# A fused two-block layer on one core: the beginning reordered, and the steps of a recurrence issued one block later

## The chip, the cores and the metric

One core of a Trainium2 chip runs the whole computation in one launch. The metric is the device time of the launch in microseconds (us), the median of several runs of the same program. The engines are TensorE (PE; PEld is its weight load), VectorE (DVE), ScalarE (ACT), GpSimd (POOL), and SyncE (SP), whose queue issues the large transfers.

## The reference, cut to what matters

The kernel computes two residual blocks in turn, on 512 tokens of 1024 channels. The change lies in the first one:

```
x' = x * rsqrt(mean(x^2) + eps) * w ;  mod = silu(c) @ ada_w + ada_b  (shift, scale, gate)
h  = x' * (1 + scale) + shift
z  = h @ w_in                      -> u_pool, g_pool, q, f_pre, i_in, g_h (1024 columns each)
f  = lb + (1 - lb) * sigmoid(f_pre) ;  k = 1 - f
o  = gated linear recurrence over 512 steps in chunks of 64, 8 heads of 128 (q, log f, k, i_in)
o  = rms_norm(o) * silu(g_h)
pool = multi-window mean of u_pool, mixed by pool_w, times silu(g_pool)
y  = [pool, o] @ w_out ;  x + gate * rms_norm(y)
```

The second block (attention, convolutions, a gated feed-forward net) follows and is not touched.

## The kernel before, in words

Everything is written out by hand: five programs (`sp_prog` L623, `pool_prog` L662, `act_prog` L788, `dve_prog` L1410, `pe_prog` L2156), one for each engine, each a fixed order of instructions with waits on semaphores. No scheduler moves anything.

**The stream.** All weights come from one array, `wstream`, whose items `stream_layout` (L32) lists in order; SP fetches them one by one into places that `place` (L283) gives: four early buffers (`EARLY`), then three `RAW` buffers in rotation. SP waits until the last user of a place is done. An item is 1 MB: either two weight blocks ("w"), or two columns of 128 of a modulation matrix ("a"). Head 0 has ten items: eight of `ada_w` and two of weights (blocks 0 and 1; 2 and 3).

**Exact products.** An fp32 product is made of three fast ones. ScalarE rounds a weight block to its high part `WH` and VectorE subtracts to get the low part `WL` (`split`, L791 and L1413). The activations have the parts `HH` and `HL` alike. `mm3` then issues high x high, high x low, low x high. A block (1024 x 128 weights) is 8 x 3 = 24 products of 512 columns. Block nb+4 is split once block nb is done (`after`), so ScalarE and VectorE go in step with TensorE.

**The beginning.** Squares of x on ScalarE (tokens' tiles 0 and 2) and VectorE (1 and 3); GpSimd takes the power -1/2; ScalarE scales x (`XLT`); TensorE transposes it; VectorE sums the modulation's items against silu(c) (`dot`, a fused multiply and sum of 1024 elements; `first_dots` L1466, `scales` L1473); ScalarE applies the modulation (`modulated`, L892) and rounds (`h_high`, L898), VectorE takes the low part (`h_low_first`, L1481). For the first four channel tiles the products of blocks 0 to 3 are plain fp32 (`plain_tile`, L2232) on the unsplit weights, then come three-part products (`first_tile`, L2239). `awake` issues small products whose result is not used: `WARM` = (12, 8) of them in two places (L2210).

**The recurrence.** Block 4h+b is head h's input b: v (0), forget gate (1), q (2), output gate (3). `head` (L852) and `gates` (L843) on ScalarE empty their banks. Head h's recurrence is a list of steps from -8 to 22, written as `hgrn(h, step)` in each engine's program: -7 transposes v; -3 makes the first product on VectorE (`Q<-HB`) and the first scores; -2 to 3 scale keys and queries level by level (levels 2 to 7: VectorE's `HB<-HB,TOT` and `Q<-Q,TOT` in turn with ScalarE's copies `PTA`, `UPA`); 5 transposes the keys and makes the scores of the six levels on TensorE, which needs level 7; 6 merges the scores; 9 output and state products; 10 the states; 13 products with the states; 14 squares (ScalarE), 15 their scale, then GpSimd's power; 16 scales the output `XL` (ScalarE), 18 transposes it, 19 gates it (`XL<-PB`, VectorE).

Which step stands where is set by two functions. Each block has four places, t = 0 to 3, behind its second, fourth, sixth and eighth channel tile:

```
def tick_of(nb, t):
    return 4 * (nb - 4) + t if nb < B_POOL else 112 + 4 * POOL_TICKS.index(nb) + t

def heads_at(nb, t):
    return [(h, tick_of(nb, t) - 16 * h) for h in range(8) if -8 <= tick_of(nb, t) - 16 * h < 23]
```

All engines follow it. On VectorE the dots of later modulation items stand at fixed (nb, t) of their own (`DOTS`, L327). Head 0's steps -8 to -1 are issued ahead of that loop.

**The pool's start** (blocks 32 on). Blocks 34 and 35 are the inputs u of pool 3; GpSimd adds shifted copies (`pool_adds`, L719; `UPA<-UPA`), VectorE and ScalarE finish them (`tail`, L1608 and L957). The last steps of head 7 fall in these blocks. GpSimd's order is written with `recur(32, 33, 34)`, the adds of the first tile, `recur(35, 36)`, the adds of the second.

Of the kernel before, what the change touches and what calls it, by code (L numbers as in the profile page):

```python
# [5 lines left out]
F32 = mybir.dt.float32  # L6
# [8 lines left out]
D = 1024  # L15
# [16 lines left out]
def stream_layout():  # L32
# [16 lines left out]
    for h in range(8):  # L49
        if h == 0:  # L50
            items += first[0:3]
        w(("w_in", 0, 0, 8, [(I0 + h * 128, 128)]), ("w_in", 0, 0, 8, [(F0 + h * 128, 128)]))
        if h:
            also()
        else:
            items += first[3:4]
        w(("w_in", 0, 0, 8, [(Q_0 + h * 128, 128)]), ("w_in", 0, 0, 8, [(GH0 + h * 128, 128)]))
        if h:
            also()
        else:  # L60
            items += first[4:8]
# [221 lines left out]
def place(n):  # L283

    if n < NEARLY:
        return ("early", n), None
    if 7 <= n < 10:
        return ("early", n - 7), n - 7
    return ("raw", n % NRAW), None if n < 7 else n - 6 if n < 13 else n - NRAW
# [81 lines left out]
def build_in(nc, ctx, A, out, consts, masks):  # L371
# [244 lines left out]
    def tick_of(nb, t):  # L616
        return 4 * (nb - 4) + t if nb < B_POOL else 112 + 4 * POOL_TICKS.index(nb) + t
# [44 lines left out]
    def pool_prog(e):  # L662
# [48 lines left out]
        for step in range(-8, 0):  # L711
            hgrn(0, step)
# [697 lines left out]
    def dve_prog(e):  # L1410
        v = Eng(e)

        def split(nb):  # L1413

            if nb >= len(BLOCKS):
                return
            n, at, size = BLOCKS[nb]
            v.wait_ge(S_.a_w, nb)
            i = nb % NW
            v.tt(WL[i][:, 0:size], raw_of(n)[:, at:at + size], WH[i][:, 0:size].bitcast(F32), SUB).then_inc(S_.v_w, nb)  # L1420
# [36 lines left out]
        for i in (1, 3):
            v.wait_ge(S_.x[i // 2], "x")
            if i > 1:
                v.wait_ge(S_.v_s, ("xsq", 1))  # L1460
            v.dot(NORM2[2], XLT[:, i, :], XLT[:, i, :], MUL, sct(0)[:, i:i + 1], scale=1.0 / D).then_inc(S_.v_s, ("xsq", i))
# [115 lines left out]
        v.wait_ge(S_.a_s, "lt")  # L1577
        v.recip(OML, LT).then_inc(S_.v_s)
        v.wait_ge(S_.v_s)
        v.tt(LT, LT, OML, MUL).then_inc(S_.v_s)  # L1580
        v.wait_ge(S_.v_s)
        v.tt(LB, LT, LT, SUB).then_inc(S_.v_s)
        v.wait_ge(S_.v_s)
        v.ts(LT, LB, 1.0, None, SUB)
        v.ts(OML, LB, -1.0, 1.0, MUL, ADD).then_inc(S_.v_s, "lb")
# [7 lines left out]
        for step in range(-8, 0):  # L1593
            hgrn(0, step)
# [561 lines left out]
    def pe_prog(e):  # L2156
# [53 lines left out]
        WARM = (12, 8)  # L2210
# [569 lines left out]
```

## Time and profile before

| | |
|---|---|
| median of 3 runs | 1124.45 us (1122.73 to 1125.68) |
| profiled execution, its own time | 1123.52 us |
| its span | 1121.7 us |
| PE busy | 1094.9 us (98%) |
| DVE, ACT, POOL busy | 792.1 (71%), 550.9 (49%), 79.1 (7%) |
| transfers | 135.54 MB, 121 GB/s mean; 419 GB/s in the stretch 3 to 34 us |
| granted TensorE clock, mean | 0.995 |

Busy time says little of TensorE, since matmuls are pipelined and their ends are modelled: what can be won is in its idle stretches. The span is what the rows are counted in; the execution's own time is 1.8 us longer.

### The profile page before, as it was taken

The page shows a single profiled execution, that of the slowest core. Times are in us where ns is not written, and L with a number is a line of the kernel's source. Part 1 is how long each engine was busy: PE and PEld are TensorE (multiplying, and loading weights), DVE is VectorE, ACT ScalarE, POOL GpSimd, SP SyncE. Part 2 cuts the span into 40 slices and gives each one's busy share as a digit, 9 for nine tenths or more (in the row PEclk, how much of TensorE's full clock was granted, in tenths as well). Part 3 has the DMA queues.
Part 4 walks back from the last instruction along what each step waited for, and adds up shares of the span by engine and source line. Part 5 has one row for each costly group of instructions (what it writes and reads, how often), then busy time and mean ns, then how long its engine had stood idle before and what let it go on. Part 6 is the DMA issues. An engine that isn't in the chain of part 4 may idle for free.

```text
span 1121.7 us, 15071 instructions
## 1 busy us (share of the span) xinstructions
PE 1094.9 (98%) x6009; PEld 891.1 (79%) x6009; DVE 792.1 (71%) x1290; ACT 550.9 (49%) x968; POOL 79.1 (7%) x115
## 2 busy tenths in 40 slices
PE   7899999999999999999999999999999999999997
PEld 4578888888888888888867666778888888888886
DVE  5876889877677747667897899786656565645427
ACT  5666565556233437764256675555444444431311
POOL 0111100111321100101000002000000000000001
PEclk9999999999999999999999999999999999999999
DMA  9653333344255754131010211022222232352211
GB/s 379 237 195 144 142 123 120 145 169 176 99 214 196 276 207 146 44 122 55 29 50 1 75 45 69 4 110 97 99 105 106 82 113 75 113 181 101 76 39 75
DMA packets 22368, 135.54 MB, mean 121 GB/s; under 512 B 2545, under 2 KB 2969, under 8 KB 8474
## 3 DMA queue, kind: packets, MB, share of 16 engines
q1 hardware_dynamic: 19936, 128.46, 31.6%
q10 hardware_dynamic: 2362, 6.12, 1.6%
q8 instruction: 47, 0.77, 0.3%
q14 instruction: 23, 0.19, 0.1%
HBM read 132.45 MB, written 2.12 MB: 120 GB/s over the span
## 4 chain that ended last, share of the span: by engine, by line
PE 90%; DVE 4%; ACT 4%; issue 1%; DMA 1%; POOL 0%; DVEq 0%; ACTq 0%; POOLq 0%
PE PB L185 89%; PE PB L193 2%; ACT WH L199 1%; DVE WL L206 1%; DMA PC<-in_params 1%; DVE HL L206 1%; ACT L200 0%; DVE EARLY L1436 0%; ACT HH L199 0%; DVE XL L214 0%; ACT PTA L200 0%; DVE CV L214 0%; ACT XL L200 0%; DVE XL L218 0%; ACT HB L200 0%
## 5 line engine op out<-in xcount | busy, mean ns | idle before, releaser
L185 PE MATMUL PB<-HH,WH 128*128 128x512 f32 (+1 forms) x880 | 338.4, 385 | 6.2 <-ACT HB L199 2.5
L185 PE MATMUL PB<-HH,WL 128*128 128x512 f32 (+1 forms) x880 | 332.6, 378 | 0.0
L185 PE MATMUL PB<-HL,WH 128*128 128x512 f32 (+1 forms) x880 | 332.5, 378 | 0.0
L206 DVE TENSOR_TENSOR WL<-RAW,WH 128x1024 fp32r<-128x1024 f32 (+2 forms) x172 | 196.5, 1148 | 190.2 <-ACT WH L199 189.7
L199 ACT ACTIVATE WH<-RAW 128x1024 fp32r<-128x1024 f32 (+2 forms) x172 | 167.7, 980 | 285.8 <-PE PB L185 267.7
L185 PEld LDWEIGHTS PB<-HH,WH 128*128 128x128 f32 x880 | 165.5, 188 | 40.9 <-ACT HB L199 2.9
L185 PEld LDWEIGHTS PB<-HH,WL 128*128 128x128 f32 x880 | 165.5, 188 | 31.3
L185 PEld LDWEIGHTS PB<-HL,WH 128*128 128x128 f32 x880 | 165.7, 188 | 29.7 <-issue 0.5
L214 DVE SCALAR_TENSOR_TENSOR CV<-VP,PC,CV 128x512 f32<-128x512 f32 x120 | 88.1, 778 | 0.7
L185 PE MATMUL PB<-WL,AH 128*128 128x512 f32 (+1 forms) x198 | 72.4, 366 | 0.0
L185 PE MATMUL PB<-WH,AH 128*128 128x512 f32 (+1 forms) x198 | 72.4, 366 | 0.0
L185 PE MATMUL PB<-WH,AL 128*128 128x512 f32 (+1 forms) x198 | 72.4, 365 | 0.0
L1436 DVE CUSTOM_DVE_ANT_0 RAW<-RAW,CR,PC 128x1024 f32<-128x1024 f32 x48 | 60.5, 1279 | 0.0
L185 PE MATMUL PB<-WH,HH 128*128 128x512 f32 x128 | 51.6, 403 | 0.3 <-DVE HL L206 0.3
L185 PE MATMUL PB<-WH,HL 128*128 128x512 f32 x128 | 50.5, 395 | 0.0
L185 PE MATMUL PB<-WL,HH 128*128 128x512 f32 x128 | 50.4, 393 | 0.0
L214 DVE SCALAR_TENSOR_TENSOR PTA<-PB,PC,PTA 128x511 f32<-128x511 f32 x66 | 49.2, 747 | 1.2
L185 PE MATMUL PB<-PTA,VG 128*128 128x512 f32 x96 | 49.5, 599 | 0.2 <-ACT PTA L200 0.2
L185 PEld LDWEIGHTS PB<-WH,AH 128*128 128x128 f32 x198 | 37.4, 189 | 6.2
L185 PEld LDWEIGHTS PB<-WL,AH 128*128 128x128 f32 x198 | 37.4, 189 | 6.1
L185 PEld LDWEIGHTS PB<-WH,AL 128*128 128x128 f32 x198 | 37.3, 188 | 6.0
L206 POOL TENSOR_TENSOR PX<-PX,NPOW 128x1 f32<-128x1 f32 (+2 forms) x8 | 7.4, 922 | 458.9 <-DVE PX L206 420.5
(293 smaller groups left out, 1692.7 us busy)
## 6 DMA issues: line engine op xcount, KB each, us to landing
RAW<-in_wstream SPq DMA_DIRECT2D x101, 1024.0 KB, 4.9
EARLY<-in_wstream SPq DMA_DIRECT2D x7, 1024.0 KB, 13.0
RAW<-in_wstream SPq DMA_DIRECT2D x5, 768.0 KB, 4.4
RAW<-in_wstream SPq DMA_DIRECT2D x5, 512.0 KB, 3.4
XL<-in_x SPq DMA_DIRECT2D x2, 1024.0 KB, 6.6
HB<-in_x SPq DMA_DIRECT2D x2, 1024.0 KB, 5.9
out<-XL SPq DMA_DIRECT2D x8, 256.0 KB, 2.0
ROWS<-in_rows ACTq DMA_DIRECT2D x3, 512.0 KB, 7.6
```

The lines of the kernel that those rows point to most:

```text
L185: return self.put(lambda e: e.matmul(o, l, r, start=start, stop=stop, skip_group_check=skip))
L193: return self.put(lambda e: e.transpose(o, i, idn))
L199: return self.put(lambda e: e.activation(o, i, f))
L206: return self.put(lambda e: e.tensor_tensor(o, a, b, op))
L214: return self.put(lambda e: e.scalar_tensor_tensor(out=o, in0=a, scalar=s, in1=b, op0=o1, op1=o2))
L1436: v.put(lambda e: e.tensor_tensor_reduce(out=PROD if vec == "cc" else w, in0=w, in1=ROW[vec], scale=1.0, scalar=col(bias, j + i), op0=MUL, ...
```

## The change

It has these parts.

- Stream: the item with blocks 0 and 1 comes third instead of fourth; the item of blocks 2 and 3 stays sixth. One `place` is adapted.
- ScalarE's beginning: a Silu on a dummy element first (it brings the table), the first square of x before silu(c), the exponential for the bounds behind the squares; a dummy Sigmoid behind the fourth high part. VectorE's: the first square of x before the bounds, the rest of the bounds behind the first scales; dots and low parts in another order.
- Blocks 0 to 3 are split only in their second half (the first is used unsplit).
- ScalarE empties block 0's bank as soon as it is done, then splits block 4, then computes the gates.
- TensorE: 3 instead of 8 products in the second `awake`; the last three-part products of blocks 0 to 3 with all high parts of the activations first.
- All steps of the recurrence stand four places (one block) later, but for head 0's first ones.

```diff
@@ stream_layout
-            items += first[0:3]
+            items += first[0:2]
         w(("w_in", 0, 0, 8, [(I0 + h * 128, 128)]), ("w_in", 0, 0, 8, [(F0 + h * 128, 128)]))
...
-            items += first[3:4]
+            items += first[2:4]
@@ place
     if 7 <= n < 10:
-        return ("early", n - 7), n - 7
+        i = (0, 1, 3)[n - 7]
+        return ("early", i), i
@@ tick_of
-        return 4 * (nb - 4) + t if nb < B_POOL else 112 + 4 * POOL_TICKS.index(nb) + t
+        return 4 * (nb - 5) + t if nb < B_POOL else 108 + 4 * POOL_TICKS.index(nb) + t
@@ in the programs of POOL, ACT, DVE, PE
-        for step in range(-8, 0):
+        for step in range(-8, -4):
             hgrn(0, step)
@@ act_prog, split (and the same in dve_prog)
-            a.copy(WH[nb % NW][:, 0:size], raw_of(n)[:, at:at + size]).then_inc(S_.a_w, nb)
+            lo_ = 512 if nb < NW else 0
+            a.copy(WH[nb % NW][:, lo_:size], raw_of(n)[:, at + lo_:at + size]).then_inc(S_.a_w, nb)
@@ act_prog, beginning
-        a.wait_ge(S_.par, "par")
-        a.wait_ge(S_.v_s, "lt")
-        a.act(LT, LT, ACTF.Exp).then_inc(S_.a_s, "lt")
+        a.wait_ge(S_.g_s, "npow")
+        a.act(NM[:, 9:10], NPOW[:, 0:1], ACTF.Silu)
...
+        x_squares(0)
         for c in range(2):
             a.wait_ge(S_.p_sm, ("c", c))
             op = a.act(ROW["c"][:, 512 * c:512 * c + 512], main.of(("z", 0, 2 + c)), ACTF.Silu)
         op.then_inc(S_.a_s, "c")
...
+        x_squares(2)
+        a.wait_ge(S_.v_s, "lt")
+        a.act(LT, LT, ACTF.Exp).then_inc(S_.a_s, "lt")
...
         h_high(2)
         h_high(3)
+        a.act(NM[:, 10:11], NPOW[:, 0:1], ACTF.Sigmoid)
...
-        Vb, Kb, Bb, Qb, Gb = head_bufs(0)
+        head(0, 0)
         split(NW)
-        a.wait_ge(S_.p_blk, 1)
-        gates(0)
-        head(0, 0)
+        head(0, 1)
+        head(0, 2)
         split(NW + 1)
-        head(0, 2)
         split(NW + 2)
@@ dve_prog, beginning
+        x_squares(1)
         v.wait_ge(S_.par, "par")
...
         first_dots(1, 0)
+        first_dots(1, 1)
+        scales(1)
         split(0)
         split(1)
-        first_dots(1, 1)
-        scales(1)
-        split(2)
         first_dots(2, 0)
         first_dots(2, 1)
         scales(2)
+        split(2)
         split(3)
         h_low_first(4)
-        first_dots(3, 0)
+        dot(FIRST_ADA[6], 0, "c")
         h_low_first(5)
+        dot(FIRST_ADA[6], 1, "c")
         first_dots(3, 1)
         scales(3)
-        h_low_first(6, 7, 0, 1, 2, 3)
+        h_low_first(0, 1, 6, 2, 7, 3)
@@ pe_prog
-        WARM = (12, 8)
+        WARM = (12, 3)
...
-        for p, bs in ((2, (0, 1)), (2, (2, 3)), (3, (1, 0)), (3, (2, 3))):
-            for k in (2 * p, 2 * p + 1):
+        for bs in ((0, 1), (2, 3)):
+            for k in (4, 5):
                 for b in bs:
                     first_tile(b, k)
+        for bs in ((1, 0), (2, 3)):
+            for k in (6, 7):
+                pe.wait_ge(S_.a_h, ("h", k))
+                for b in bs:
+                    pe.mm(zs[b], WH[b][:, js(k)], hh(k), False, False)
+                    pe.mm(zs[b], WL[b][:, js(k)], hh(k), False, False)
+            for k in (6, 7):
+                pe.wait_ge(S_.v_h, ("h", k))
+                for b in bs:
+                    op = pe.mm(zs[b], WH[b][:, js(k)], hl(k), False, k == 7)
```

Three places show what the table of steps does to an engine's order.

VectorE from the splits of blocks 5 to 7 on, before. `Q<-HB` is head 0's first product, `HB<-HB` and `Q<-Q` its levels, `RAW,PX` a dot, `WL<-RAW` a split:

```order
L206 TENSOR_TENSOR WL<-RAW,WH 128x1024 x3
L206 TENSOR_TENSOR Q<-HB 128x512
L206 TENSOR_TENSOR HB<-HB 128x256
L206 TENSOR_TENSOR Q<-Q,HB 128x256
L206 TENSOR_TENSOR HB<-HB,TOT 128x128x2
L206 TENSOR_TENSOR Q<-Q,TOT 128x128x2
L234 COPY_PREDICATED AT<-MK,PB 128x512
L206 TENSOR_TENSOR HB<-HB,TOT 128x64x4
L206 TENSOR_TENSOR Q<-Q,TOT 128x64x4
```

The same place with the change:

```order
L206 TENSOR_TENSOR WL<-RAW,WH 128x1024 x3
L206 TENSOR_TENSOR Q<-HB 128x512
L1442 ISA RAW,PX<-RAW,GP,PC 128x1024
L1442 ISA PX 128x1
L206 TENSOR_TENSOR HB<-HB 128x256
L206 TENSOR_TENSOR Q<-Q,HB 128x256
L206 TENSOR_TENSOR HB<-HB,TOT 128x128x2
L206 TENSOR_TENSOR Q<-Q,TOT 128x128x2
L234 COPY_PREDICATED AT<-MK,PB 128x512
L1442 ISA RAW,PX<-RAW,GP,PC 128x1024
L1442 ISA PX 128x1
L206 TENSOR_TENSOR WL<-RAW,WH 128x1024
```

Two dots and the split of block 8 now stand ahead of level 4 (`128x64x4`), which follows the last row.

ScalarE, around the gate of head 0 (the Silu behind the table load, then two rows of the modulation, then the split of block 8), before:

```order
L199 ACTIVATE UPA<-HB 128x8x32
L199 ACTIVATE UPA<-Q 128x8x32
L200 ACT_TABLE_LOAD
L200 ACTIVATE HB<-PB 128x512
L200 ACTIVATE XL<-XL 128x1024
L200 ACTIVATE CR<-CR 128x1024
L199 ACTIVATE WH<-RAW 128x1024
```

With the change:

```order
L199 ACTIVATE PTA<-HB 128x64x4
L199 ACTIVATE PTA<-Q 128x64x4
L200 ACT_TABLE_LOAD
L200 ACTIVATE HB<-PB 128x512
L200 ACTIVATE XL<-XL 128x1024
L200 ACTIVATE CR<-CR 128x1024
L199 ACTIVATE WH<-RAW 128x1024
L199 ACTIVATE HB<-PB 128x512
L199 ACTIVATE UPA<-HB 128x32x8
```

The group stood behind the last copies of the levels (`128x8x32`) and stands now behind level 3's (`128x64x4`), in front of the rest.

ScalarE at the pool's start, before. `UPA<-PB` empties a block u, `XR,SCT<-PB` are head 7's squares, `XL<-PB,SCT` its scaling, `DH<-UPA` the tail of a pool tile, `GP<-PB` a gate:

```order
L199 ACTIVATE UPA<-PB 128x512
L200 ACTIVATE XL<-PB,SCT 128x128 x4
L199 ACTIVATE WH<-RAW 128x256
L200 ACTIVATE GP<-PB 128x512
L199 ACTIVATE DH<-UPA 128x512
```

With the change:

```order
L199 ACTIVATE UPA<-PB 128x512
L197 ACTIVATE XR,SCT<-PB 128x128 x4
L199 ACTIVATE WH<-RAW 128x256
L200 ACTIVATE GP<-PB 128x512
L199 ACTIVATE DH<-UPA 128x512
L200 ACTIVATE XL<-PB,SCT 128x128 x4
```

The scaling stood ahead of the second tile's tail and stands behind it; the squares moved from ahead of the first tile's tail to behind it.

## Rows read from the trace of the kernel before

**Rows 1.** The page's chain of waits that ended last, by engine.

```profile
PE 90%; DVE 4%; ACT 4%; issue 1%; DMA 1%; POOL 0%; DVEq 0%; ACTq 0%; POOLq 0%
```

**Rows 2.** Issues: SP's timeline (start, length), and issues with KB and us to landing.

```profile
16.37 0.33 SPq L182 DMA_DIRECT2D EARLY<-in_wstream  x1
...
EARLY<-in_wstream SPq DMA_DIRECT2D x1, 1024.0 KB, 12.9
...
RAW<-in_wstream SPq DMA_DIRECT2D x1, 1024.0 KB, 4.7
```

**Rows 3.** Timelines of DVE and ACT, head 0: start, us, engine, line, operation [idle].

```profile
60.82 0.41 DVE L206 TENSOR_TENSOR HB<-HB,TOT 128x256 f32<-128x256 f32 x1
61.79 0.42 DVE L206 TENSOR_TENSOR HB<-HB,TOT 128x256 f32<-128x256 f32 x1 [0.22 <-ACT UPA L199]
62.47 1.28 DVE L1436 CUSTOM_DVE_ANT_0 RAW<-RAW,GP,PC 128x1024 f32<-128x1024 f32 x1
69.66 1.23 DVE L206 TENSOR_TENSOR WL<-RAW,WH 128x1024 fp32r<-128x1024 f32 x1 [3.04 <-ACT WH L199]
...
64.89 1.28 ACT L200 ACT_TABLE_LOAD   x1
68.58 1.05 ACT L199 ACTIVATE WH<-RAW 128x1024 fp32r<-128x1024 f32 x1
```

**Rows 4.** Timeline of DVE, the scales of channels 4, 5 and of 6, 7.

```profile
34.39 0.16 DVE L214 SCALAR_TENSOR_TENSOR PX<-PX,PC 128x2 f32<-128x2 f32 x1
42.34 0.16 DVE L214 SCALAR_TENSOR_TENSOR PX<-PX,PC 128x2 f32<-128x2 f32 x1
```

**Rows 5.** Timelines of ACT and PE, from the last high part to block 4.

```profile
44.73 0.63 ACT L199 ACTIVATE HH<-AT 128x512 fp32r<-128x512 f32 x1
49.03 1.28 ACT L200 ACT_TABLE_LOAD   x1
52.91 1.05 ACT L199 ACTIVATE WH<-RAW 128x1024 fp32r<-128x1024 f32 x1
...
53.06 0.50 PE L185 MATMUL PB<-HH,WH 128*128 128x512 f32 x1 [2.49 <-ACT HB L199]
```

**Rows 6.** Timeline of PE, blocks 4 and 5, and head 0's transposes.

```profile
57.82 0.40 PE L185 MATMUL PB<-HL,WH 128*128 128x512 f32 x1
...
64.19 0.39 PE L185 MATMUL PB<-HH,WL 128*128 128x512 f32 x1
65.13 0.66 PE L193 MATMUL PB<-IDN,HB 128*128 128x128 f32 x4 [0.55 <-DVE HB L206]
```

**Rows 7.** Stretches: us, busy of each engine, PEclk, DMA share, GB/s.

```profile
18.00:22.00 4.00, 3.72 (x17) 3.07 (x18) 3.33 (x7) 3.43 (x5) 0.00 (x0) 0.57 1.01 422
52.00:54.00 2.00, 0.94 (x4) 0.81 (x5) 0.83 (x2) 2.00 (x4) 1.23 (x3) 1.00 0.02 4
704.00:708.00 4.00, 4.00 (x12) 3.08 (x12) 3.59 (x14) 2.59 (x4) 1.33 (x1) 0.57 0.00 0
```

**Rows 8.** Timelines of DVE and PE, head 3: its last level and its transposes.

```profile
184.48 0.41 DVE L206 TENSOR_TENSOR HB<-HB,TOT 128x256 f32<-128x256 f32 x1
...
186.26 0.60 PE L193 MATMUL PB<-IDN,HB 128*128 128x128 f32 x4
```

**Rows 9.** Timelines of PE, ACT and POOL, head 7 at the pool's start.

```profile
293.76 1.09 PE L185 MATMUL PB<-SS,E 128*64 128x128 f32 x14
301.71 0.60 PE L193 MATMUL PB<-IDN,XL 128*128 128x128 f32 x4
...
294.89 0.28 ACT L197 ACTIVATE XR<-PB 128x128 f32<-128x128 f32 x1 [2.13 <-PE PB L185]
300.31 1.14 ACT L200 ACTIVATE XL<-PB,SCT 128x128 f32<-128x128 f32 x4
...
297.98 1.02 POOL L206 TENSOR_TENSOR SCT<-SCT,NPOW 128x4 f32<-128x4 f32 x1
300.49 4.69 POOL L206 TENSOR_TENSOR UPA<-UPA 128x512 f32<-128x512 f32 x4 [1.50 <-ACT UPA L199]
```

More of the change, by code:

```diff
@@ L876, in act_prog, with x_squares @@
         a.dma(IDN[:, :], consts[:, 0:128]).then_inc(S_.idn, "idn", by=16)
-        a.wait_ge(S_.par, "par")
-        a.wait_ge(S_.v_s, "lt")
-        a.act(LT, LT, ACTF.Exp).then_inc(S_.a_s, "lt")
+        a.wait_ge(S_.g_s, "npow")
+        a.act(NM[:, 9:10], NPOW[:, 0:1], ACTF.Silu)
+        def x_squares(i):
+            a.wait_ge(S_.x[i // 2], "x")
+            a.act(NORM2[i // 2], XLT[:, i, :], ACTF.Square, scale=2.0 ** -5, acc=sct(0)[:, i:i + 1]).then_inc(S_.a_s, ("xsq", i))
+        x_squares(0)
         for c in range(2):
@@ L883, in act_prog @@
         op.then_inc(S_.a_s, "c")
-        for i in (0, 2):
-            a.wait_ge(S_.x[i // 2], "x")
-            a.act(NORM2[i // 2], XLT[:, i, :], ACTF.Square, scale=2.0 ** -5, acc=sct(0)[:, i:i + 1]).then_inc(S_.a_s, ("xsq", i))
+        x_squares(2)
+        a.wait_ge(S_.v_s, "lt")
+        a.act(LT, LT, ACTF.Exp).then_inc(S_.a_s, "lt")
         for i in range(4):
@@ L927, in act_prog @@
         a.dma(ROW["c2"], A["rows"][:, 2 * D:3 * D]).then_inc(S_.crow, "cr", by=16)
-        Vb, Kb, Bb, Qb, Gb = head_bufs(0)
+        head(0, 0)
         split(NW)
-        a.wait_ge(S_.p_blk, 1)
-        gates(0)
-        head(0, 0)
+        head(0, 1)
+        head(0, 2)
         split(NW + 1)
-        head(0, 2)
         split(NW + 2)
         split(NW + 3)
-        for step in range(-8, 0):
+        for step in range(-8, -4):
             hgrn(0, step)
@@ L1418, in split @@
             v.wait_ge(S_.a_w, nb)
-            i = nb % NW
-            v.tt(WL[i][:, 0:size], raw_of(n)[:, at:at + size], WH[i][:, 0:size].bitcast(F32), SUB).then_inc(S_.v_w, nb)
+            i, lo_ = nb % NW, 512 if nb < NW else 0
+            v.tt(WL[i][:, lo_:size], raw_of(n)[:, at + lo_:at + size], WH[i][:, lo_:size].bitcast(F32), SUB).then_inc(S_.v_w, nb)
         def after(nb):
@@ L1451, in lo, with x_squares @@
             v.tt(dst, src, hi.bitcast(F32), SUB).then_inc(S_.v_h, name)
+        def x_squares(i):
+            v.wait_ge(S_.x[i // 2], "x")
+            v.dot(NORM2[2], XLT[:, i, :], XLT[:, i, :], MUL, sct(0)[:, i:i + 1], scale=1.0 / D).then_inc(S_.v_s, ("xsq", i))
+        x_squares(1)
         v.wait_ge(S_.par, "par")
@@ L1456, in dve_prog @@
         v.tt(LT, hlb, hlb, SUB).then_inc(S_.v_s, "lt")
[L1457 to L1461, printed above, removed]
+        v.wait_ge(S_.v_s, ("xsq", 1))
+        x_squares(3)
         v.wait_ge(S_.a_s, ("xsq", 2))
@@ L1487, in dve_prog @@
         scales(0)
+        v.wait_ge(S_.a_s, "lt")
+        v.recip(OML, LT).then_inc(S_.v_s)
+        v.wait_ge(S_.v_s)
+        v.tt(LT, LT, OML, MUL).then_inc(S_.v_s)
+        v.wait_ge(S_.v_s)
+        v.tt(LB, LT, LT, SUB).then_inc(S_.v_s)
+        v.wait_ge(S_.v_s)
+        v.ts(LT, LB, 1.0, None, SUB)
+        v.ts(OML, LB, -1.0, 1.0, MUL, ADD).then_inc(S_.v_s, "lb")
         first_dots(1, 0)
+        first_dots(1, 1)
+        scales(1)
         split(0)
         split(1)
-        first_dots(1, 1)
-        scales(1)
-        split(2)
         first_dots(2, 0)
@@ L1496, in dve_prog @@
         scales(2)
+        split(2)
         split(3)
         h_low_first(4)
-        first_dots(3, 0)
+        dot(FIRST_ADA[6], 0, "c")
         h_low_first(5)
+        dot(FIRST_ADA[6], 1, "c")
         first_dots(3, 1)
         scales(3)
-        h_low_first(6, 7, 0, 1, 2, 3)
+        h_low_first(0, 1, 6, 2, 7, 3)
         def hgrn(h, step):
@@ L1575, in hgrn @@
                     .then_inc(S_.v_ax, ("dg", h))
[L1577 to L1585, printed above, removed]
         first = LATER_ADA[0]
+        split(NW)
         dot(first, 0, "c")
-        split(NW)
         dot(first, 1, "c")
@@ L1592, in dve_prog @@
             split(NW + n)
-        for step in range(-8, 0):
+        for step in range(-8, -4):
             hgrn(0, step)
@@ L2242, in first_tile @@
             pe.wait_ge(S_.v_h, ("h", k))
-            op = pe.mm3(zs[b], wh[:, js(k)], wl[:, js(k)], hh(k), hl(k), False, k == 7)
-            if k == 7:
-                op.then_inc(S_.p_blk, b)
+            pe.mm3(zs[b], wh[:, js(k)], wl[:, js(k)], hh(k), hl(k), False, False)
         pe.wait_ge(S_.c, "c")
@@ L2267, in pe_prog @@
                 x_tiles(6, 7)
-        for p, bs in ((2, (0, 1)), (2, (2, 3)), (3, (1, 0)), (3, (2, 3))):
-            for k in (2 * p, 2 * p + 1):
+        for bs in ((0, 1), (2, 3)):
+            for k in (4, 5):
                 for b in bs:
                     first_tile(b, k)
+        for bs in ((1, 0), (2, 3)):
[8 more added lines that the diff above has]
+                    op = pe.mm(zs[b], WH[b][:, js(k)], hl(k), False, k == 7)
+                    if k == 7:
+                        op.then_inc(S_.p_blk, b)
         def hgrn(h, step):
@@ L2346, in tick @@
                     if nb == 4 and t == 0:
-                        for step in range(-8, 0):
+                        for step in range(-8, -4):
                             hgrn(0, step)
```

## The prediction, on record before the changed kernel ran

> **What bounds the kernel now.** The view of the chain that ended last comes first: TensorE (PE) carries 90% of it, VectorE (DVE) and ScalarE (ACT) 4% each [rows 1]. The change adds and removes next to no TensorE work, so it can only move waits of TensorE. The timelines of each engine show where these are. The first 38 us are preparation: x, norm, modulation. Then come the four products of head 0 (blocks 0 to 3), and from 53.06 us on the stream of blocks, where TensorE is never idle but for short gaps. I read the timelines in the order of the three edits: the beginning, the recurrence of head 0, and the end of the recurrence at head 7.
>
> **Part 1, the beginning.** Both reorderings of x (ScalarE's first square before its tables, VectorE's first square before the bounds) bring the norm's scale about 3 us forward. That alone ends nothing: the later channels wait for the modulation weights, which land one after another. The fifth pair to be summed needs the item that landed 12.9 us after its issue at 16.37, at 29.3 us [rows 2]. Its place in the stream is unchanged and the queue in front of it is as long, so it lands at 29.3 again. In the kernel before VectorE was behind it: two dots of 1.28 us, 2.4 for both since they overlap a little [rows 3], and the scales at 34.39 [rows 4]. After, VectorE has lost work ahead of it (half of the first four splits, halves of 1.22 us) and waits for the landing: 29.3 + 2.4 + 0.2 = 31.9. From there to the last scales it was 42.34 - 34.39 = 7.95 us [rows 4], and the moved halves and low parts make it 7.9 in my count. So the modulation is done 2.5 us earlier, and ScalarE's last high part, which started at 44.73 and took 0.63 [rows 5], ends at 42.86. TensorE has no work left when it comes: the second weights land two items (2.5 us each, 1 MB at some 420 GB/s) before 29.3, at 24.3, and the 16 plain products start the second pair then. They wait about 1.2 us for it, end near 35.5, and the 24 products of channels 4 and 5 near 41. Behind that high part stand 20 products (4 high, 4 low, 12 of the other pair). The pace is (64.19 - 57.82) / 28 = 0.2275 us [rows 6]; 20 of them and a restart are 4.65. The first four blocks end at 47.6 where they ended at 53.06 - 2.49 = 50.57 [rows 5]: **3.0 us earlier**.
>
> Block 4 waited those 2.49 us because ScalarE split block 4, loaded a table and computed the gates before it emptied the first bank. From the load at 49.03 to the split of block 5 at 52.91 are 3.88 us [rows 5]: 1.28 the load, 2.6 gates and copy. The change moves the table load to an idle place and empties the bank first. Block 0 ends with the eighth of the 20 products and is seen done at 45.1; copy 0.5, split 0.95, VectorE's low part 1.22 with two hand-overs of 0.1 give 48.0. TensorE waits 0.4 us instead of 2.49, and block 4 starts **5.1 us earlier**.
>
> **Part 2, the recurrence of head 0, one block later.** Before, TensorE reached the transposes of head 0 at 65.13, in the middle of block 5, after a wait of 0.55 [rows 6]. Now they stand in the middle of block 6, 24 products later, so 65.13 + 24 x 0.2275 = 70.6 is the time that would be no gain. TensorE could be there at 48.0 + 60 x 0.2275 + 1.2 (four transposes, the first scores, restarts) = 62.9. VectorE decides whether it may go on. Its order has three new things in front of the last factors: the first dot of the next item right behind head 0's first product, a second dot, and the split of block 8.
> The chain: from 45.1, copy, split, gates, copy (0.5 + 0.95 + 2.1 + 0.5) and the split of block 5 end at 50.2 on ScalarE; VectorE's part ends at 51.5 and frees the buffer of the next item. This lands 4.7 us after its issue [rows 2], at 56.2. The dot ends at 57.5. Levels 2 and 3 with ScalarE's copies take 2.2: one level is 61.79 - 60.82 = 0.97 [rows 3]. At 59.7 ScalarE turns to head 0's gate: table load, Silu, two rows of 1024, and only then the split of block 8, 68.58 - 64.89 = 3.69 us later [rows 3]. In the kernel before that stood behind the recurrence's factors and cost nothing. So the split runs from 63.4 to 64.45, VectorE's part starts 1.08 behind its start as at 69.66 [rows 3] and gives way to level 4 at 65.6. Three levels at 0.97 and one product of 0.42 end at 69.0. **TensorE waits 6.1 us in block 6 and goes on at 69.05, 1.5 us earlier than no gain.** Of the 5.1 us and of head 0's own waits that the shift was to save, all but 1.5 are given back.
> **A rule weighed.** The load at 64.89 is 1.28 us, and the 3.69 us to the split hold just it and the three activations, so 1.3 stands in the chain [rows 3]. The Trainium skill (ScalarE: Activation LUTs, What ACT_TABLE_LOAD costs) gives a switch a drain of about 1.4 us more, 2.66 in all. By it the wait would be 7.5 and nearly nothing of the gain be left. The trace has no such drain.
>
> **The clock.** An idle TensorE loses its clock here: the granted clock was 0.57 in 18 to 22 us, behind the wait for x, and in 704 to 708; it stayed 1.00 around the 2.49 us of block 4 [rows 7]. Such a mean is a stretch at the lower level, 1.2 GHz, and the rest at 2.4. A wait of 6.1 us is over twice the longest that kept it, so I expect the fall. At 704 to 708 the share lost is 4 x (1 - 0.57) = 1.7 us [rows 7]. Here the first 3.4 us are small score products; bounds 0.4 (they don't feel it) and 3.0 (the low level outlasts them). I take 1.5, as in the nearest row.
> The same rows bear on the warm-up products cut from 8 to 3. The Trainium skill (TensorE: Matmul & The Clock Gate, Part 1) says that the low clock is the default and activity lifts it, which speaks against the cut. The first plain tiles at half rate would cost up to 1.7 us; 1.2 of it falls in the wait for the second weights, so 0 to 0.6, taken as 0.
>
> **Part 3, heads 1 to 6.** Head 3's last factor ended at 184.48 + 0.41, TensorE came at 186.26: 1.4 us of room [rows 8]. The new order puts a table load and Silu (1.8 us) between levels 3 and 4 where there were none; the same order lets levels 1 to 3 run 0.5 to 0.7 earlier, since one dot less stands before them. Left is 0.2 us of room in heads 2 to 5, and 1.2 more in heads 1, 6 and 7, which have no dot between levels 5 and 6. Cost 0; bounds 0 and 1.
>
> **Part 4, head 7 at the pool's start.** Here the shift crosses an order that was not shifted. The chain before: state products at 293.76, squares 294.89, GpSimd's power 297.98 (1.02), its adds for the second pool tile 300.49 (4.69), and ScalarE's scaling at 300.31 (1.14), all ahead of the transposes at 301.71, which waited for nothing [rows 9]. GpSimd's adds and the scaling were side by side. After, the power of head 7 stands ahead of the adds as before, but ScalarE's scaling stands behind the tail that waits for these adds. So, from the end of the state products (293.76 + 1.09 in the old count [rows 9]): squares 1.1, sum 0.3, power 1.05, adds 4.7, VectorE's tail 0.9, ScalarE's copy 0.6 (512 columns, as the 0.63 at 44.73 [rows 5]), scaling 1.15: 9.8 us. TensorE does 12 products, and 18 of the next block, 30 x 0.2275 + 0.1 = 6.9 us. **A new wait of 2.8 us**; bounds 2 and 3.5, by what of the small ends overlaps.
>
> **Sum**, against the profiled execution of 1123.52: -1.5 + 1.5 + 0 + 2.8 = +2.8. That execution is 0.9 under the median of 1124.45. On the median it is 1127.2. A measurement of this kernel can't tell less than 0.3% (3.4 us) from no change, so below 1121.1 is faster and above 1127.8 slower; my forecast is the upper end of "same".
>
> **Rivals.**
> A, the beginning's gain is kept (0.15): VectorE isn't held in front of level 4. For it: ScalarE has idle stretches then, and the items may land earlier. Against: both engines work in order. With no wait in block 6 it gains 70.6 - 62.95 = 7.6, loses 2.8: 1119.6.
> B, the wait of head 7 doesn't come (0.16), since GpSimd's adds finish sooner or the order hides them: 1124.4, no change. Against it stand five durations in rows.
> C, slower by the clock (0.12): the low level lasts the full 3.0 in block 6 and also comes in head 7's wait of 2.8 us, another 1.7. It decides once that wait is longer than what keeps the clock; 2.49 kept it once. 1124.45 - 1.5 + 3.0 + 2.8 + 1.7 = 1130.4.
> D, slower by heads 2 to 5 (0.10): the 0.2 us of room is my count. If the dot between levels 5 and 6 falls fully into the path, each loses 1.0: 1131.
> E, the forecast (0.47), 1126.1 to 1128.7 by the clock's bounds.
> Faster is A: 0.15. Slower is C, D and a third of E: 0.37. The rest, 0.48, is no change. The range 1120.0 to 1130.5 leaves out the far parts of A and D.
>
> **What would show it.** Block 4 starts near 48 us. TensorE's longest wait is one of about 6 us near 63 to 69 for VectorE's HB product, and behind it the granted clock is 0.50. The waits of heads 1 to 6 are under 0.3. Near 307 us TensorE waits 2.8 us for ScalarE's XL. If block 6 has no such wait, the forecast is wrong on the fast side; if heads 2 to 5 show waits of 0.5 or more, on the slow side.

## The result, and the profile after

The changed kernel takes **1131.84 us** (median of 4 runs, 1131.43 to 1134.19) against 1124.97 us for the kernel before (4 runs beside it, 1122.73 to 1125.68). The ratio is 1.0069, 95% interval 1.0049 to 1.0089: slower by 0.7%. The prediction was 1127.2 with a range to 1130.5. The result lies above it, 0.8 over rival D's time and 1.4 over rival C's. By its mechanism it is nearest to C, as shown below.

The profiled execution took 1131.85 us with a span of 1130.0; its span is 8.3 us longer than that of before. The page's chain of waits that ended last, by engine, answers to [rows 1]:

```profile
PE 81%; DVE 7%; ACT 5%; DMA 3%; issue 2%; POOL 1%; SPq 0%; DVEq 0%; ACTq 0%; POOLq 0%
```

TensorE's share has fallen from 90% to 81%: the chain now leaves it in several places. The timeline of PE (start, length, engine, line, operation, and in brackets the idle time before it with what ended it) shows them, rows from the beginning to the pool's start:

```profile
47.83 0.47 PE L185 MATMUL PB<-HH,WH 128*128 128x512 f32 x1 [0.26 <-DVE WL L206]
52.32 0.69 PE L185 MATMUL PB<-HB 128*64 128x64 f32 x16 [1.04 <-ACT HB L199]
...
69.39 1.11 PE L193 MATMUL PB<-IDN,HB 128*128 128x128 f32 x4 [5.27 <-DVE HB L206]
70.44 2.78 PE L185 MATMUL PB<-PTA 128*64 128x32 f32 x48
73.02 2.75 PE L185 MATMUL PB<-UPA 128*64 128x32 f32 x48
75.71 0.80 PE L185 MATMUL PB<-HH,WH 128*128 128x512 f32 x1
76.30 0.63 PE L185 MATMUL PB<-HL,WH 128*128 128x512 f32 x1
...
80.57 0.55 PE L185 MATMUL PB<-HH,WL 128*128 128x512 f32 x1
80.95 0.40 PE L185 MATMUL PB<-HH,WH 128*128 128x512 f32 x1
...
282.49 0.65 PE L193 MATMUL PB<-IDN,XL 128*128 128x128 f32 x4 [0.88 <-ACT XL L200]
...
314.88 0.66 PE L193 MATMUL PB<-IDN,XL 128*128 128x128 f32 x4 [2.90 <-ACT XL L200]
...
379.79 0.47 PE L185 MATMUL PB<-WH,MPH 128*128 128x512 f32 x1 [0.29 <-DVE HB L214]
```

The same timeline of before has these rows around head 0:

```profile
56.87 0.69 PE L185 MATMUL PB<-HB 128*64 128x64 f32 x16 [1.71 <-ACT HB L199]
...
68.63 0.50 PE L185 MATMUL PB<-HH,WH 128*128 128x512 f32 x1
...
71.48 0.39 PE L185 MATMUL PB<-HH,WH 128*128 128x512 f32 x1
```

- Block 4 starts at 47.83 where it started at 53.06 [rows 5]: 5.2 us are won.
- The waits up to head 0's transposes were 1.71 (before the first scores at 56.87) and 0.55 [rows 6]; they are 1.04 and 5.27: 4.05 us are lost.
- From the transposes to the product behind the scores are 75.71 - 69.39 = 6.32 us, and the next 12 products take until 80.95: 5.24 us. Before it was 3.50 (65.13 to 68.63) and 2.85 (68.63 to 71.48). 5.2 us are lost without any wait.
- 0.9 us at 282.49 (head 6), 2.9 at 314.88 (head 7), 0.3 at 379.79.

Together -5.2 + 4.05 + 5.2 + 0.9 + 2.9 + 0.3 = +8.15 of the 8.3. Where the 5.2 us without a wait went is seen in the clock. The stretches of after (us, busy of each engine, PEclk, DMA share, GB/s):

```profile
18.00:22.00 4.00, 4.00 (x14) 2.03 (x15) 2.87 (x5) 2.52 (x5) 0.00 (x0) 1.00 1.00 418
64.00:66.00 2.00, 0.13 (x1) 0.00 (x0) 1.15 (x2) 1.30 (x2) 0.00 (x0) 1.00 0.73 307
66.00:68.00 2.00, 0.00 (x0) 0.00 (x0) 1.57 (x6) 1.33 (x4) 0.00 (x0) 0.81 0.00 0
78.00:80.00 2.00, 2.00 (x6) 1.61 (x5) 1.13 (x2) 0.00 (x0) 0.00 (x0) 0.50 0.03 8
80.00:82.00 2.00, 2.00 (x8) 1.58 (x8) 0.00 (x0) 0.79 (x1) 0.00 (x0) 0.78 0.77 246
```

The granted clock falls to 0.50 (1.2 GHz) in the wait, near 67.2, and comes back near 80.9, after 11.5 us of unbroken work. In it a product of 512 columns takes (80.57 - 76.30) / 10 = 0.427 us instead of 0.2275. The Trainium skill (TensorE: Matmul & The Clock Gate, Part 1) gives 426.7 ns for such a product at the low clock; the trace agrees. At 18 to 22 us the clock is 1.00 where it was 0.57 [rows 7]: the five warm-up products less cost nothing that shows here. x also comes earlier, and no run separates the two.

### The profile page after: what moved, and what is told of

Same layout as the page of the kernel before. It is cut to its first block, busy times and chain, and to the rows that moved or that the text cites. A ratio compares the mean times of both kernels' runs of the same rounds, so it can differ in the third digit from the quotient of the medians.

```text
span 1130.0 us, 15053 instructions
## 1 busy us (share of the span) xinstructions
PE 1097.8 (97%) x5999; PEld 891.9 (79%) x5999; DVE 792.1 (70%) x1290; ACT 550.4 (49%) x970; POOL 83.2 (7%) x115
## 4 chain that ended last, share of the span: by engine, by line
PE 81%; DVE 7%; ACT 5%; DMA 3%; issue 2%; POOL 1%; SPq 0%; DVEq 0%; ACTq 0%; POOLq 0%
PE PB L185 80%; DMA RAW<-in_wstream 3%; PE PB L193 2%; ACT WH L199 1%; DVE RAW L1442 1%; POOL UPA L206 1%; DVE WL L206 1%; DVE EARLY L1442 1%; ACT HH L199 0%; DVE XL L214 0%; SPq L182 0%; ACT L200 0%; DVE UPA L214 0%; DVE HB L206 0%; ACT PTA L200 0%
## 5 line engine op out<-in xcount | busy, mean ns | idle before, releaser
L206 DVE TENSOR_TENSOR WL<-RAW,WH 128x1024 fp32r<-128x1024 f32 (+3 forms) x172 | 195.6, 1144 | 199.3 <-ACT WH L199 198.7
L199 ACT ACTIVATE WH<-RAW 128x1024 fp32r<-128x1024 f32 (+3 forms) x172 | 166.6, 975 | 281.4 <-PE PB L185 270.5
## 6 DMA issues: line engine op xcount, KB each, us to landing
EARLY<-in_wstream SPq DMA_DIRECT2D x7, 1024.0 KB, 13.7
```

The source lines that it names most:

```text
L199: return self.put(lambda e: e.activation(o, i, f))
L206: return self.put(lambda e: e.tensor_tensor(o, a, b, op))
```

## Why the wait in block 6 is 5.3 us

VectorE and ScalarE up to the last factor of head 0 (timelines of DVE and ACT of after):

```profile
56.62 1.28 DVE L1442 CUSTOM_DVE_ANT_0 RAW<-RAW,GP,PC 128x1024 f32<-128x1024 f32 x1 [1.81 <-DMA RAW<-in_wstream]
64.85 1.23 DVE L206 TENSOR_TENSOR WL<-RAW,WH 128x1024 fp32r<-128x1024 f32 x1 [3.40 <-ACT WH L199]
65.99 0.42 DVE L206 TENSOR_TENSOR HB<-HB,TOT 128x256 f32<-128x256 f32 x1
68.92 0.42 DVE L206 TENSOR_TENSOR HB<-HB,TOT 128x256 f32<-128x256 f32 x1 [0.22 <-ACT UPA L199]
...
60.09 1.28 ACT L200 ACT_TABLE_LOAD   x1
61.38 0.60 ACT L200 ACTIVATE HB<-PB 128x512 f32<-128x512 f32 x1
63.77 1.04 ACT L199 ACTIVATE WH<-RAW 128x1024 fp32r<-128x1024 f32 x1
```

VectorE waits 1.81 us for an item, then 3.40 us for ScalarE's split of block 8, which stands behind the gate group of head 0 (60.09 to 63.77: 3.68 us). The four levels behind it are in time only at 69.34. This is the chain that the prediction worked out, within 0.4 us. Behind the load the Silu starts 0.01 us after its end; the drain that the Trainium skill (ScalarE: Activation LUTs, What ACT_TABLE_LOAD costs) adds does not show here either.

## The experiments

All were run in five rounds beside the kernel before, whose median was 1123.88 (e1 to e4), 1123.76 (e5 to e8) and 1123.68 us (e9, e10).

**e1: the steps back in their places, the new beginning kept.**

```diff
-        return 4 * (nb - 5) + t if nb < B_POOL else 108 + 4 * POOL_TICKS.index(nb) + t
+        return 4 * (nb - 4) + t if nb < B_POOL else 112 + 4 * POOL_TICKS.index(nb) + t
-        for step in range(-8, -4):
+        for step in range(-8, 0):
```

> The changed kernel with the recurrence's steps back in their old places; the new beginning is kept. Theory (the later steps make the loss, the beginning is a gain): block 4 starts at 47.8 us as in the changed kernel, head 0's transposes come in block 5 near 59 us (48.87 + 9.8 of TensorE work, VectorE's last factor held by the item that lands at 56.6), against 65.13 before, and no wait over 0.3 us stands in the pool's first blocks. Time 1119.5, between 1118 and 1122, that is 5.5 under before. Rival (the new beginning is paid back later by itself: half splits, the table loads, the moved item): 1124 to 1126.

Measured: 1120.52 (1118.51 to 1122.22, 6 runs), ratio 0.9968 [0.9957, 0.9980]. **Faster than before by 0.3%.** The timeline of PE:

```profile
47.85 0.47 PE L185 MATMUL PB<-HH,WH 128*128 128x512 f32 x1 [0.27 <-DVE WL L206]
52.35 0.69 PE L185 MATMUL PB<-HB 128*64 128x64 f32 x16 [2.46 <-ACT HB L199]
61.56 0.66 PE L193 MATMUL PB<-IDN,HB 128*128 128x128 f32 x4 [1.46 <-DVE HB L206]
...
368.57 0.47 PE L185 MATMUL PB<-WH,MPH 128*128 128x512 f32 x1 [0.41 <-DVE HB L214]
```

Of the 5.2 us at block 4 head 0 takes 1.6 back (61.56 against 65.13: 3.6 are left). Its transposes come 2.6 us later than the 59 that I expected, since the first scores wait 2.46 us and the transposes 1.46. At the first product of the mixes (`PB<-WH,MPH`, where the pool's tiles are mixed) 3.0 us are left (368.57 against 371.56), and by the medians 3.4 at the end. The profiled span is 4.3 us shorter, but in this run the clock did not fall near 704 as it did before [rows 7]. So the beginning is a gain, and the loss belongs to the steps.

**e2: the kernel before with only the steps later** (the lines of e1 the other way round).

> The kernel before with only the recurrence's steps one block later. Theory: the same three waits as in the changed kernel: block 6 (TensorE is there at 69.4, VectorE's last factor near 72.8: 3.4 us), head 6 in block 33 (0.9), head 7 in block 37 (2.9), and the clock, which costs nothing if 3.4 us keep it and up to 5.0 if they do not. 1124.97 + 2.9 + 4.2 = 1132 with the clock kept, 1137 with it lost. Rival (the steps are harmless by themselves and only collide with the new beginning): 1125.

Measured: 1135.48 (1134.33 to 1135.73, 4 runs), ratio 1.0099 [1.0086, 1.0112]. The timeline of PE:

```profile
73.06 1.12 PE L193 MATMUL PB<-IDN,HB 128*128 128x128 f32 x4 [4.54 <-DVE HB L206]
...
285.16 0.66 PE L193 MATMUL PB<-IDN,XL 128*128 128x128 f32 x4 [0.88 <-ACT XL L200]
317.56 1.04 PE L193 MATMUL PB<-IDN,XL 128*128 128x128 f32 x4 [2.90 <-ACT XL L200]
```

The same three waits. The first is 4.54 where I worked out 3.4, and the clock is lost with it. The transposes of 0.66 that take 1.04 at 317.56 show that here it is lost at head 7 too. The steps alone cost 11.6 us and the beginning alone gains 3.4: the sum is 8.2, the two together measured 6.9 to 8.0 more than before (by which median of before is taken). By these medians the two parts hardly touch each other.

**e3: the gate group behind the level copies.** ScalarE's `head(0, 3)` (load, Silu, two rows) moves behind the copies of block 5.

```diff
                 recur(4 * h + b)
-                if b == 0:
+                if b == (1 if h == 1 else 0):
                     head(h - 1, 3)
```

> The changed kernel with ScalarE's group for head 0's output gate (table load, Silu, two rows) behind the level copies of block 5 and behind the split of block 8. Theory (the group holds the split of block 8 and so level 4, and the clock falls because of the wait that this makes): the wait in block 6 shrinks from 5.27 to about 1.7 us, the granted clock stays 1.00 from 60 to 90 us, and 3.6 + 5.0 = 8.6 us come back: 1123.3, between 1121.5 and 1125. Rival (the item that lands at 56.6 and the dot that waits for it make the wait): the wait stays over 4 us, the clock falls, and the time is 1130 or more.

Measured: 1125.45 (1123.00 to 1127.86, 12 runs), ratio 1.0011 [1.0000, 1.0022]. The wait is as expected, the clock is not. PE and the stretches behind it:

```profile
66.05 0.66 PE L193 MATMUL PB<-IDN,HB 128*128 128x128 f32 x4 [1.77 <-DVE HB L206]
```

```profile
66.00:68.00 2.00, 1.95 (x38) 1.78 (x38) 0.33 (x1) 1.99 (x3) 0.00 (x0) 0.79 0.00 0
68.00:70.00 2.00, 2.00 (x43) 2.00 (x42) 0.00 (x0) 2.00 (x3) 0.00 (x0) 0.50 0.00 0
```

Five of the twelve runs had a mean clock of 0.997 and took 1123.00 to 1123.31, the 1123.3 of the theory. The other seven had 0.992 to 0.995 and took 1124.83 to 1127.86. The profiled one is among them: in it the clock fell after a wait of only 1.77 us, and again at head 7's wait, from 309 to 313. The transposes, the scores and the 12 products behind them took 9.45 us (66.05 to 75.50), where before took 6.35: 3.1 us for the first fall. So the group made 3.5 of the 5.27 us, and the clock's price is paid or not from run to run.

**e4: the wait filled with products whose result is not used.**

```diff
                 bk = take_aux(("kt", h), 0)
+                for _ in range(22 if h == 0 else 0):
+                    pe.mm(bk[:, :], WH[2][:, js(0)], hh(0), True, True)
```

> The changed kernel with 22 products of 512 columns, whose result is not used, in front of head 0's transposes: TensorE is busy for 5.0 of the 5.27 us that it waits. Theory (the idle stretch makes the clock fall, and that costs 5.0 us: transposes, scores and 12 products at about half pace until 80.9): the wait shows as 0.3 us, the granted clock stays 1.00, 1131.84 - 5.0 = 1126.9. My prediction took 1.5 for it: 1130.3. Rival (the clock falls because transposes and small scores follow, whatever stands before them): it falls all the same, 1131.8.

Measured: 1128.24 (1126.64 to 1129.76, 5 runs), ratio 1.0037 [1.0025, 1.0049]. PE, then its stretches:

```profile
69.50 0.65 PE L193 MATMUL PB<-IDN,HB 128*128 128x128 f32 x4 [0.34 <-DVE HB L206]
...
309.86 1.02 PE L193 MATMUL PB<-IDN,XL 128*128 128x128 f32 x4 [2.91 <-ACT XL L200]
```

```profile
68.00:70.00 2.00, 1.66 (x10) 1.04 (x8) 1.52 (x4) 1.77 (x4) 0.00 (x0) 1.00 0.00 0
74.00:76.00 2.00, 2.00 (x10) 1.62 (x10) 1.97 (x3) 0.16 (x1) 1.84 (x3) 1.00 0.86 356
...
310.00:312.00 2.00, 2.00 (x8) 1.71 (x8) 1.77 (x4) 0.00 (x0) 0.00 (x0) 0.50 0.00 0
312.00:314.00 2.00, 2.00 (x7) 1.60 (x6) 0.88 (x2) 0.46 (x1) 0.00 (x0) 0.65 0.26 33
```

The transposes come no earlier (69.50 instead of 69.39), and yet 3.6 us are won. The transposes and scores are the same as in after and the clock holds through them, so in block 6 it is the idle stretch that makes it fall. The missing 1.4 of the 5.0 us stand at head 7: there the clock falls now, for 2 x 0.50 + 2 x 0.35 = 1.7 us. The one run with a mean clock of 0.997 took 1126.64, near the 1126.9 of the theory; by its mean it kept the clock there, though no trace of it was kept.

**e5: head 7's scaling ahead of the pool's tail** (ScalarE).

```diff
             pool_gate(p, 0, nb)
+            recur(nb + 1)
             tail(p + 1, 1)
-            recur(nb + 1)
```

> The changed kernel with ScalarE's scaling of head 7 ahead of the tail of the second pool tile (recur(37) before tail(3, 1)). Theory (the scaling waits only because it stands behind the tail, which waits for GpSimd's adds): the wait of 2.9 us near 315 is gone, and with it the occasional fall of the clock there. 1131.84 - 2.9 = 1128.9, between 1127.5 and 1129.5. Rival (the power or GpSimd's queue makes the wait): it stays, 1131.8.

Measured: 1131.21 (1130.57 to 1132.08, 5 runs), ratio 1.0068 [1.0054, 1.0082]. The wait of 2.9 us is gone and the time hardly moved. It comes back further on, by the timeline of PE:

```profile
346.69 0.47 PE L185 MATMUL PB<-HH,WH 128*128 128x512 f32 x1 [0.52 <-DVE WL L206]
352.75 0.47 PE L185 MATMUL PB<-HH,WH 128*128 128x512 f32 x1 [0.36 <-DVE WL L206]
372.86 0.47 PE L185 MATMUL PB<-HH,WH 128*128 128x512 f32 x1 [0.81 <-DVE WL L206]
379.14 0.47 PE L185 MATMUL PB<-WH,MPH 128*128 128x512 f32 x1 [0.56 <-DVE HB L214]
```

2.25 us of new waits for VectorE, where after had the one of 0.29. From head 6's transposes at 282 to the first product of the mixes it takes 96.96 us (282.18 to 379.14), where after took 97.30. My expectation of 1128.9 was wrong by a second bound that stood just under the first.

**e6: e3 with 6 products of the kind of e4** (22 becomes 6), so that 0.4 us of the 1.77 are left.

> The gate group behind block 5's copies, as in e3_gate_behind, and 6 products with unused result in front of head 0's transposes, so that of the 1.77 us of waiting 0.4 is left. In e3 five runs of twelve had a mean clock of 0.997 and took 1123.0 to 1123.3, seven had 0.992 to 0.995 and took 1124.8 to 1127.9. Theory (even 1.8 us of waiting, followed by small products, puts the clock at risk; filled, it does not): most runs at 0.995 or higher, median 1123.3, spread under 2.5 us, what is left of it from the 2.9 us of head 7. Rival (the falls are chance or come elsewhere): the same two groups, median 1125.5.

Measured: 1124.35 (1122.86 to 1126.09, 11 runs), ratio 1.0006 [0.9997, 1.0015]. The spread is 3.2 us instead of 4.9, and three runs in eleven reach 0.997. The median is 1.1 under that of e3, half of what I expected: in the profiled run the clock held in block 6 and fell at head 7's 2.90 us instead, as in e4.

**e7: four orders mended.** e3 and e5, and besides VectorE's dot that waits for the item at 56.6 behind levels 2 and 3, and head 6's scaling ahead of the table load.

```diff
@@ VectorE
-                    dots(nb, t)
+                    if (nb, t) == (4, 3):
+                        dots(4, 1)
+                    if (nb, t) != (4, 1):
+                        dots(nb, t)
@@ ScalarE, block 32 (and the step left out in block 33)
             if m == 0:
+                hgrn(6, 16)
                 head(7, 3)
```

> The changed kernel with four orders mended: gate group behind block 5's copies, VectorE's dot of the item that lands at 56.6 behind levels 2 and 3, head 6's scaling ahead of the table load in block 32, head 7's ahead of the tail. Theory: none of the waits of 5.3, 0.9 and 2.9 us is left, the clock stays 1.00 from 24 us on, 1131.84 - 5.3 - 5.0 - 0.9 - 2.9 = 1117.7, between 1116.5 and 1119.5: 6.5 under before, more than the beginning with the old steps (1120.5). Rival (a dot held back delays the stream, or the table load now stands in another head's way): over 1120.

Measured: 1122.02 (1121.78 to 1123.68, 11 runs), ratio 0.9989 [0.9980, 0.9997]. That is 4.3 us more than expected. Head 0's wait is down to 0.66 and the clock holds through it. Head 6's wait of 0.88 is gone, but head 7's transposes now wait 0.78: ScalarE's scaling, load and Silu (from 268.53 on) hold its split of a block until 271.46, VectorE waits 2.56 us for it, and the last levels stand behind that. So that move won 0.1 us. The pool's stages show the waits of e5 again, and GpSimd's timeline shows where they start:

```profile
64.92 0.66 PE L193 MATMUL PB<-IDN,HB 128*128 128x128 f32 x4 [0.66 <-DVE HB L206]
...
277.54 0.63 PE L193 MATMUL PB<-IDN,HB 128*128 128x128 f32 x4 [0.78 <-DVE HB L206]
...
363.52 0.47 PE L185 MATMUL PB<-HH,WH 128*128 128x512 f32 x1 [0.83 <-DVE WL L206]
369.97 0.47 PE L185 MATMUL PB<-WH,MPH 128*128 128x512 f32 x1 [0.76 <-DVE HB L214]
```

```profile
296.90 1.02 POOL L206 TENSOR_TENSOR SCT<-SCT,NPOW 128x4 f32<-128x4 f32 x1 [5.93 <-DVE SCT L211]
297.89 4.79 POOL L206 TENSOR_TENSOR UPA<-UPA 128x512 f32<-128x512 f32 x4
```

The input of the adds (`UPA<-UPA`) was in place at 293.07 + 0.58 (ScalarE's copy of the block). GpSimd stands in front of head 7's power for 5.93 us and starts them 4.2 us late. In the profiled run the clock also fell for 6.8 us near 701, twice as long as in the kernel before (see the last section). Then VectorE's tail, dots, the fetch that the dots release, the splits and the gates of the mixes follow one another.

**e8: ScalarE's order around block 4 as before, on top of e1** (no Sigmoid in the pause; split, gates with the load, then block 0's bank).

> The kernel with the steps back (e1_steps_back, 1120.52), and in addition ScalarE's order around block 4 as before: split of block 4, the table load, the gates, then block 0's bank, and no Sigmoid in the pause. Theory (that order made 2.1 us of the 5.2 us by which block 4 starts earlier): block 4 starts at 49.9 instead of 47.85, the wait before it is 2.3 us. Head 0's transposes come later by less, since they waited 1.46 us there: 1120.5 to 1122.6, taken as 1121.8. Rival (the wait moves and nothing is lost): 1120.5.

Measured: 1121.23 (1120.65 to 1122.81, 11 runs), ratio 0.9979 [0.9970, 0.9988]. Block 4 starts at 50.09 behind a wait of 2.43 us, 2.2 later than in e1, and head 0's transposes come at 62.14, only 0.6 later. The order is worth 2.2 us at block 4 and 0.6 to 0.7 in the end.

**e9: e7 with GpSimd's adds ahead of head 7's power.**

```diff
                 if p == 3 and m == 1:
-                    recur(35, 36)
+                    recur(35)
                 if p == 2 and m == 0:
-                    recur(37)
+                    recur(36, 37)
```

> The kernel of e7_all_orders (1122.0, where 1117.7 was expected), and GpSimd's adds for the second pool tile ahead of head 7's power. In e7 these adds could start at 293.65 and start at 297.89, since GpSimd stands waiting for head 7's sum; VectorE's tail, its dots, the fetch behind them (4.7 us) and the splits follow in one chain, and TensorE waits 0.42, 0.35, 0.83 and 0.76 us for it from 337 to 370. Theory (the pool stages have a second bound right under TensorE, and the later steps lengthen it by these 4.3 us): the waits between 300 and 380 are gone, 1122.0 - 2.4 = 1119.6, between 1118 and 1120.5. Rival (the waits come from the stream itself, which cannot bring the items sooner): they stay, 1122.

Measured: 1120.23 (1118.67 to 1120.58, 5 runs), ratio 0.9962 [0.9948, 0.9976]. GpSimd's timeline:

```profile
293.79 4.68 POOL L206 TENSOR_TENSOR UPA<-UPA 128x512 f32<-128x512 f32 x4 [2.76 <-ACT UPA L199]
298.42 1.02 POOL L206 TENSOR_TENSOR SCT<-SCT,NPOW 128x4 f32<-128x4 f32 x1
```

TensorE has no wait of 0.3 us left from 278 to 467 us; the 0.78 at 277.6 stays, and so does head 0's, now 0.64. With the orders mended the later steps are no longer slower: 1120.2, the same as the 1120.5 of e1. In the profiled runs e9 is even 1.8 us ahead at the first product of the mixes (366.77 against 368.57), and loses more than that near 700, where its clock falls for 6.8 us and that of e1 does not. So whether the later steps, in good order, gain anything isn't shown.

**e10: after with both orders at head 7** (e5 and the lines of e9).

> The changed kernel with both orders at head 7 mended: ScalarE's scaling ahead of the tail (e5_head7_order alone: 1131.2, its wait of 2.9 us gone and 2.3 us of waits for VectorE's splits and gates in its place, 346 to 380), and GpSimd's adds ahead of the power. Theory: none of the two kinds of wait is left, 1131.84 - 2.9 - 0.3 = 1128.6, between 1127.8 and 1129.3. Rival (the waits behind 340 have another source): 1131.

Measured: 1128.08 (1127.28 to 1129.72, 5 runs), ratio 1.0039 [1.0026, 1.0051]. ScalarE's order alone brought 0.6 us, both together 3.8. The low stretch of the clock in block 6 was shorter here (back at 78.1 instead of 80.9), so I take the stretch behind it: from head 6's transposes to the first product of the mixes are 93.75 us (281.27 to 375.02), against 96.96 in e5 and 97.30 in after. There ScalarE's order brings 0.3 us and both 3.55.

GpSimd's order alone was not run, and it is a rival for the wait of 2.9 us too. An estimate from rows of after: the input of the adds is in place at 303.18 (ScalarE's copy, 302.60 + 0.58), and they start at 307.42. Moved ahead of the power they would end near 307.9 and the power near 308.9. With the 0.96 and 0.53 us that the tail took there, the scaling would start near 309.4 and end near 310.5, ahead of TensorE at 311.98. By this the one move would have taken away the visible wait and the bound under it.

## Why the prediction was wrong

**Part 1, right.** Block 4 at 47.83 against 48.0.

**Part 2, right in its mechanism, 0.3 us short.** I had the wait at 6.1 us, ending at 69.05; it was 5.27, ending at 69.39, since TensorE arrived near 64.1 and not at 62.9: the wait of 1.04 us for the first scores was not in my sum. "All but 1.5 are given back": all but 1.2. e3 shows that the gate group makes 3.5 us of the wait, e7 that the dot in front of level 2 makes 1.1 of the rest.

**The clock, the step that failed.** The fall came as expected, but I took 1.5 us for it, with 3.0 as the upper bound. It cost 5.2 in the profile, and e4 gives 3.6 (its median) to 5.2 (its fastest run). Three readings were wrong. The price was copied from a stretch of 4 us [rows 7], though nothing said that this fall would be as short; it lasted 13.7 us. The lower bound rested on small products that don't feel the clock: transposes and scores took 6.32 us instead of 3.50, so they feel it nearly in full. And the row of 704 to 708 is no idle TensorE: it works there without a gap, as the last section shows, so this row could give neither the cause nor the length of a fall behind a wait. This term alone is 3.7 of the 5.5 us by which the profiled executions differ more than the 2.8 of the sum.

**Part 3, right for heads 1 to 5.** In the chain of waits the same stretch of six heads runs from 84.29 to 265.44, 181.15 us, and before from 75.05 to 256.31, 181.26 us; rival D did not come. Head 6 was missed: its scaling stands in block 33 behind head 7's load, Silu, a split and a gate, and costs 0.9 (in e7, which moves it ahead of the load, this wait is gone). I had read the room of the levels there and not the order of ScalarE in front of the scaling.

**Part 4, right: 2.9 against 2.8** (the terms, 9.8 and 6.9, make 2.9 themselves). What I didn't see was under it. GpSimd's power stood ahead of the adds before, too, but now its sum comes a block later, and the adds stand 4.2 us behind their input. I had this in the chain of the scaling and not in the chain of the pool's next weights. There it cost little in the changed kernel, where TensorE was late anyway, and takes 2.25 us back when only ScalarE's order is mended (e5; e7 has the same waits).

**The sum** by the measured terms: -1.2 + 5.2 - 0.1 + 0.9 + 2.9 + 0.3 = +8.0, against 8.3. Of the rivals C had the right cause. That its clock terms (3.0 + 1.7) come close to the 5.2 is luck: it was one longer fall and none at head 7. D's 1131, nearer still, is luck altogether, since heads 2 to 5 didn't wait. The range to 1130.5 left out D's own value and not only its far part.

## What to carry to other kernels

A wait of TensorE that may cost its clock is priced as the work that follows it at half pace, small transposes and scores included, until the clock is seen to return: here 5.2 us behind a wait of 5.27, as much as the wait itself. The price varies: 3.9 in e10 behind a wait of 5.43 (69.53 to 79.74 for what takes 6.35), 3.1 in e3 behind one of 1.77. When steps of one engine are moved past a table, ask for every in-order engine what now stands behind a waiting instruction: the long waits here came from an order that had been right for the old places, and e9 takes the waits of 5.27, 0.88 and 2.90 us down to 0.64, 0.78 and none by moving five calls and no arithmetic. And a wait that is taken away shows the next bound only when it is gone, so follow the time behind it and not the wait.

## What was not expected of the hardware

The length of a wait alone doesn't say whether the clock falls. It stayed 1.00 around 2.49 us at block 4 in the kernel before [rows 7], around 2.46 and 1.46 in e1, and around 2.90 at 314.88 in after. It fell after 1.77 us in the profiled run of e3, after 2.91 in that of e4, and around 2.43 in e8, where this stretch has 0.74:

```profile
48.00:52.00 4.00, 1.91 (x5) 1.53 (x6) 2.67 (x5) 3.97 (x7) 2.13 (x4) 0.74 0.00 0
```

It can also fall without any wait. The stretch of 704 to 708 in before [rows 7] stands behind 3.5 us in which TensorE worked without a gap, on 32 products of one column each (timeline of PE of before, the first eight of them):

```profile
700.30 0.94 PE L185 MATMUL PB<-ONES,DG 128*128 128x1 f32 x8
```

All twelve profiled kernels run these products. In eight the clock fell at them or right behind them for 3.4 us, in e7, e9 and e10 for 6.8 us, and in e1 not at all (1.00 from 700 to 708). None of the changes touches this place, and at half pace it makes up to 3 us between profiled runs: the profiled e9 leads e1 by 1.8 us at the first product of the mixes and ends 1.2 behind it.

One program does both: in e3 five runs took 1123.0 to 1123.3 and seven 1124.8 to 1127.9. Two runs of such a kernel can differ by 0.4% with nothing else changed, and the mean clock beside each run goes with it. What decides it within a run stays open; no experiment here was made for it.
